# Input tiles outside, token thirds inside, in the first output tile of six late products

## The chip, the cores and the metric
The kernel runs on one core of a Trainium2 chip. The metric is the device time of one execution in microseconds (us); less is better. Engines are named PE (TensorE), DVE (VectorE), ACT (ScalarE), POOL (GpSimd) and SP (SyncE, which issues DMAs here).

## What is computed
One inference step of a hybrid decoder layer over 1024 prompt tokens and 8 sample tokens, 1032 in all, with D = 1024 and a hidden width of 4096. After the two mixers come memory cross-attention and a squared-ReLU MLP, and these last parts are where the change lies:

```python
def cross_attn(h, mk, mv, w_cq, w_co):
    q = (h @ w_cq).reshape(Bsz, L, X_HEADS, X_HEADDIM)
    ...
    return o @ w_co

x = x + merged @ w_out
x = x + cross_attn(rmsnorm(x, g_x), mk, mv, w_cq, w_co)
hf = rmsnorm(x, g_ff) @ w_ff_up
x = x + jnp.square(jax.nn.relu(hf)) @ w_ff_down
```

## The kernel before
Activations are kept transposed: a tensor of 1032 tokens is 8 **input tiles** of 128 channels by 1032 tokens. A product takes a 128x128 block of weights as the stationary operand and writes an **output tile** of 128 channels. Since a PSUM bank holds 512 columns, the 1032 tokens go in three **thirds** of 344, each in its own bank (0, 1, 2). To keep accuracy, weights and activations are both split into a high and a low part, and each product of a weight block and a third is three matmuls (high by high, high by low, low by high: lines 1293, 1294, 1295). An output tile is thus 3 thirds x 8 input tiles x 3 = 72 matmuls, and a product of 8 output tiles is 576.

The late products in program order, all made by `project_all` and its inner `project3`, are named here **CQ** (query projection), **CO** (attention output), and then for each quarter q of the hidden width **FUq** (up) and **FDq** (down), q = 0 to 3. Output tiles are called tile 0 to tile 7 of their product, input tiles go by k = 0 to 7.

- `project3(it, base, before, ...)` makes two output tiles, u = 0 and 1. It waits for the split weights of the tile (`w_split`, from POOL, lines 2768 and 2769). For each third n it waits until the bank has been emptied of the tile before (`before(u, n)`), then goes through k = 0 to 7. The last matmul of a third raises `proj_full`.
- Only tile 0 of a product can meet input tiles that aren't finished yet. `ready(k)` is a semaphore wait for each k, made in the first third; CQ and FU0 have it, on `xl_ready`. FD0 to FD3 instead wait ahead of the whole product until 7 of the 8 hidden tiles are there (`h_ready`, line 1377), and for the eighth at k = 7 (`late`). CO has no such wait.
- `xl_ready` is raised by DVE in `residual_tile` (line 2446: the low part of the scaled residual tile), after adding a square into a running sum (line 2443). `h_ready` is raised by DVE in `low` (line 2600), which ends this chain for hidden tile j: ACT empties the three banks with a ReLU (`relu`, line 1859), DVE scales and squares (`square`, lines 2594 and 2595), ACT makes the high part (`high`, line 1864), DVE the low part.
- The banks of FU are emptied by ACT (`proj_taken`), those of CO and FD by DVE adds into the residual (`sum_taken`, lines 2577 and 2621), those of CQ by ACT.
- In FU0 two small pieces of PE work for the norm stand behind the first and second pair of output tiles (`beside`). Because of the norm, the squares of FU0 begin only after its fourth tile, so that its hidden tiles are finished late, while in FU1 to FU3 they follow each output tile.

Each engine executes its own queue in order, and the matmuls' order is the order in which these loops are written.

Of the kernel before, what the change touches and what calls it, by code (L numbers as in the profile page):

```python
# [11 lines left out]
P = 128  # L12


def wait(eng, sem, value):

    if isinstance(value, int) and value <= 0:
        return
    eng.wait_ge(sem, value)


class Banks:
# [20 lines left out]
    def before(self, name, it=0):  # L43
        b, n = self.place[name]
        return self.base[b] + it * self.per[b] + n
# [9 lines left out]
def rounded(ap):  # L55

    return ap.bitcast(F32R)
# [26 lines left out]
def hybrid_step(nc, io):  # L84
# [10 lines left out]
    KT = D // P  # L95
    NC = T // P
    NG = 3
    GW = NT // NG
# [26 lines left out]
    with ExitStack() as ctx:  # L125
# [6 lines left out]
        def sem(name):  # L132
            return ctx.enter_context(nc.semaphore(name))
# [62 lines left out]
        psum = ctx.enter_context(nc.psum_tensor("psum", [P, 8, 512], F32))  # L196
# [3 lines left out]
        proj_full = sem("proj_full")  # L200
# [34 lines left out]
        sum_taken = sem("sum_taken")  # L235
# [24 lines left out]
        hr_ready, h_ready = sem("hr_ready"), sem("h_ready")  # L260
# [154 lines left out]
        def part(buf, at_, n):  # L415
# [13 lines left out]
        wh, wl = ([wparts[:, (2 * part_ + i) * KT * P:(2 * part_ + i + 1) * KT * P] for i in range(2)]  # L429
                  for part_ in range(2))  # L430
# [23 lines left out]
        hlowv, hiddenv, xFv = (t.rearrange("p (k t) -> p k t", k=KT) for t in (hlow, hidden, xF))  # L454
# [396 lines left out]
        def _(pe):  # L851
# [96 lines left out]
            for n in range(3):  # L948
                hand(setup_plan, f"sc{n}", 0, lambda bk, n=n: (
                    pe.matmul(bk[0:72, 0:GW], wsc[:, k, :], xnv[:, k, n * GW:(n + 1) * GW],  # L950
                              start=(k == 0), stop=(k == KT - 1)) for k in range(KT)))
# [15 lines left out]
            for j in range(2):  # L967
                hand(setup_plan, f"csr{j}", 0, lambda bk, j=j: (
                    pe.matmul(bk[0:40, i * P:(i + 1) * P], tok72[:, 4 * j + i, 0:40], triu[:, :],
                              start=True, stop=True) for i in range(4)))  # L970
# [4 lines left out]
                          start=True, stop=True) for i in range(SH_N // 2)))  # L975
# [254 lines left out]
            with pe.Fori(1, KT // 2) as pair:  # L1230
                j = pair * 2
# [41 lines left out]
                    pe.transpose(cols(bk, 2 * i + t), Ktok[:, t, (2 * q + i) * P:(2 * q + i + 1) * P], ident[:, :])  # L1273
                    for i in range(2) for t in range(MT)))

            def project3(it, base, before, hi, lo, ready=None, late=None):


                for u in range(2):
                    slot = (base + u) % 2  # L1280
                    pe.wait_ge(w_split, it + (base - W_SPLIT + u + 1))
                    for n in range(3):
                        wait(pe, *before(u, n))
                        for k in range(KT):
                            if u == 0 and n == 0:
                                if ready is not None:
                                    pe.wait_ge(*ready(k))
                                if late is not None and k == KT - 1:
                                    pe.wait_ge(*late)
                            w_hi, w_lo = (rounded(w[slot][:, k * P:(k + 1) * P]) for w in (wh, wl))  # L1290
                            x_hi, x_lo = (rounded(x[:, k, n * GW:(n + 1) * GW]) for x in (hi, lo))
                            out = psum[:, n, 0:GW]
                            pe.matmul(out, w_hi, x_hi, start=(k == 0), stop=False)  # L1293
                            pe.matmul(out, w_hi, x_lo, start=False, stop=False)  # L1294
                            mm = pe.matmul(out, w_lo, x_hi, start=False, stop=(k == KT - 1))  # L1295
                        mm.then_inc(proj_full, 1)

            def project_all(base, before, hi, lo, ready=None, late=None, beside=()):
                for i in range(max(1, len(beside))):
                    project3(2 * i, base, lambda u, n: before(2 * i, u, n), hi, lo, ready if i == 0 else None,  # L1300
                             late if i == 0 else None)
                    if beside:
                        beside[i]()
                with pe.Fori(max(1, len(beside)), KT // 2) as pair:
                    j = pair * 2
                    project3(j, base, lambda u, n: before(j, u, n), hi, lo)


            pe.wait_ge(proj_taken, A_CQ)
            project_all(W_CQ, lambda j, u, n: (proj_taken, 3 * j + (A_CQ + 3 * u + n - 2)), xBv, xlowv,  # L1310
                        ready=lambda k: (xl_ready, k + 1))
            pe.wait_ge(q8s_ready, 1)
# [6 lines left out]
            with pe.Fori(0, XH_N) as h:  # L1319
# [10 lines left out]
                for s in range(2):  # L1330
# [10 lines left out]
                    for k in range(2):  # L1341
# [12 lines left out]
                        for k in range(KT) for t in range(MT)))  # L1354
            taken(G, "os1", XH_N - 1)
            project_all(W_CO, lambda j, u, n: (sum_taken, 3 * j + (V_CO + 3 * u + n - 2)), atBv, atv)


# [12 lines left out]
            for q in range(FQ_N):  # L1371
                base, v0, a0 = W_FU + 2 * KT * q, V_FU + V_Q * q, A_END + A_Q * q
                project_all(base, lambda j, u, n: (sum_taken, v0 - 2 + n) if isinstance(j, int) and j + u == 0 else
                            (proj_taken, 3 * j + (a0 + 3 * u + n - 2)), xFv, xlowv,
                            ready=(lambda k: (xl_ready, KT + k + 1)) if q == 0 else None,
                            beside=(ff_sums, ff_spread) if q == 0 else ())
                pe.wait_ge(h_ready, KT * q + KT - 1)
                project_all(base + KT, lambda j, u, n: (proj_taken, a0 + A_Q - 2 + n) if isinstance(j, int) and j + u == 0 else
                            (sum_taken, 3 * j + (v0 + 3 * u + n - 2)), hiddenv, hlowv, late=(h_ready, KT * q + KT))

            pe.wait_ge(xacc_done, 3 * (KT - 1))
            hand(G, "zst", 0, lambda bk: stats([xnv[:, 0, :]], NT, bk, 0, 1))
# [1461 lines left out]
```

## Time and profile before

| | |
|---|---|
| time, median of 3 runs | 3988.59 us (3986.17 to 3994.87) |
| time of the profiled execution | 3986.69 us |
| its span | 3985.0 us |
| PE busy | 3647.3 us (92%), 20671 matmuls |
| DVE, ACT, POOL busy | 43%, 21%, 21% |
| PE on the chain that ended last | 78% |

The span is what the trace covers; the profiled execution's own time is 1.7 us longer. "Busy" is the time an engine spent in instructions. Matmuls are pipelined: a matmul of 0.32 us begins about 0.157 us after the one before it, so that start-to-start distances, not durations, give PE's pace. The granted clock is that which the chip allows TensorE, 1.00 being 2.4 GHz and 0.50 being 1.2 GHz. The late products, from CO on, fill the span from 3098 us to 3955 us; CQ starts at 2812 us.

### The profile page before, as it was taken

How to read it: one execution, taken by the hardware profiler on the slowest of the kernel's cores; microseconds unless marked ns; L12 is line 12 of the kernel's file. 1: busy time of each engine (PE TensorE's matmuls, PEld its weight loads, DVE VectorE, ACT ScalarE, POOL GpSimd, SP SyncE). 2: the span in 40 equal slices, each digit the busy share in tenths (PEclk: the TensorE clock that was granted, in tenths of full speed). 3: DMA queues.
4: the chain of work that ended last, by engine and by line, in shares of the span. 5: the costliest groups of instructions: out<-in, count | busy, mean ns of one | idle time of the engine just before them, and what ended most of it. 6: DMA issues, size and time to landing. Idle time of an engine off the chain costs nothing.

```text
span 3985.0 us, 53368 instructions
## 1 busy us (share of the span) xinstructions
PE 3647.3 (92%) x20671; PEld 3128.8 (79%) x20671; DVE 1693.9 (43%) x2840; ACT 842.6 (21%) x1709; POOL 850.5 (21%) x389
## 2 busy tenths in 40 slices
PE   6899999998899999999999968999988998999998
PEld 5888898887899766666666655667955998999998
DVE  4656555566200356566665760112044232313133
ACT  4333233333211022122221110011123110101010
POOL 3222323232122000000000000000422443444442
PEclk7999999998899998999999979999987999999999
DMA  3111101111222122212222135112312111111111
GB/s 112 45 44 39 32 26 38 43 38 33 75 76 78 54 63 81 81 49 68 66 78 78 43 106 187 54 46 79 128 57 74 43 47 42 43 48 48 43 43 64
DMA packets 317893, 248.31 MB, mean 62 GB/s; under 512 B 11028, under 2 KB 293213, under 8 KB 317717
## 3 DMA queue, kind: packets, MB, share of 16 engines
q1 hardware_dynamic: 282798, 211.28, 17.4%
q10 hardware_dynamic: 34992, 35.58, 2.5%
q8 instruction: 74, 1.21, 0.1%
q14 instruction: 29, 0.24, 0.0%
HBM read 200.50 MB, written 46.78 MB: 62 GB/s over the span
## 4 chain that ended last, share of the span: by engine, by line
PE 78%; DVE 10%; issue 4%; ACT 3%; DMA 2%; POOL 1%; ACTq 0%; DVEq 0%; SPq 0%; POOLq 0%
PE psum L894 22%; PE psum L1293 8%; PE psum L1295 8%; PE psum L1294 8%; PE psum L912 4%; PE psum L913 4%; PE psum L914 4%; PE psum L1028 2%; PE psum L1036 2%; PE psum L1040 2%; PE psum L868 2%; PE psum L1186 1%; PE psum L1324 1%; PE psum L1260 1%; PE psum L1352 1%
## 5 line engine op out<-in xcount | busy, mean ns | idle before, releaser
L894 PE MATMUL psum<-xn,slab 128*128 128x344 f32 x2688 | 823.8, 464 | 29.2 <-ACT arena L1684 17.8
L894 PEld LDWEIGHTS psum<-xn,slab 128*128 128x128 f32 x2688 | 513.5, 194 | 304.0 <-issue 37.6
L2768 POOL TENSOR_SCALAR wparts<-slab 128x1024 fp32r<-128x1024 f32 x80 | 221.9, 2773 | 1001.2 <-POOLq L68 1001.2
L912 PE MATMUL psum<-xh,whe 128*128 128x344 f32 x1152 | 393.4, 341 | 16.2 <-POOL wle L2689 12.8
L913 PE MATMUL psum<-xl,whe 128*128 128x344 f32 x1152 | 373.5, 324 | 0.0
L914 PE MATMUL psum<-xh,wle 128*128 128x344 f32 x1152 | 373.0, 324 | 0.0
L1293 PE MATMUL psum<-at,wparts 128*128 128x344 f32 x960 | 310.8, 324 | 30.0 <-DVE r L2600 26.3
L1295 PE MATMUL psum<-at,wparts 128*128 128x344 f32 x960 | 309.5, 322 | 0.0
L1294 PE MATMUL psum<-xlow,wparts 128*128 128x344 f32 x960 | 307.5, 320 | 0.0
L2689 POOL TENSOR_TENSOR wle<-slab,whe 128x1024 fp32r<-128x1024 f32 x56 | 137.7, 2459 | 721.5 <-ACT whe L1435 721.5
L894 PE MATMUL psum<-arena,slab 128*128 128x344 f32 x768 | 229.1, 460 | 26.6 <-DMA arena<-d_yb 18.5
L1293 PE MATMUL psum<-hB,wparts 128*128 128x344 f32 x768 | 246.7, 321 | 4.5 <-DVE xlow L2446 4.5
L1294 PE MATMUL psum<-r,wparts 128*128 128x344 f32 x768 | 247.4, 322 | 0.0
L1295 PE MATMUL psum<-hB,wparts 128*128 128x344 f32 x768 | 245.7, 320 | 0.0
L912 PEld LDWEIGHTS psum<-xh,whe 128*128 128x128 f32 x1152 | 223.6, 194 | 18.2 <-POOL wle L2689 13.6
L2753 POOL TENSOR_TENSOR arena<-arena 128x1024 f32<-128x1024 f32 x16 | 30.0, 1898 | 972.8 <-DMA arena<-in_state_ssm_dram 972.8
L894 PEld LDWEIGHTS psum<-arena,slab 128*128 128x128 f32 x768 | 148.5, 194 | 105.2 <-issue 31.4
L1916 DVE SCALAR_TENSOR_TENSOR arena<-arena 128x1024 f32<-128x1024 f32 x168 | 224.6, 1337 | 2.7
L913 PEld LDWEIGHTS psum<-xl,whe 128*128 128x128 f32 x1152 | 223.2, 194 | 0.0
L914 PEld LDWEIGHTS psum<-xh,wle 128*128 128x128 f32 x1152 | 221.7, 192 | 0.0
L2769 POOL TENSOR_TENSOR wparts<-slab,wparts 128x1024 fp32r<-128x1024 f32 x80 | 206.5, 2581 | 6.7
L1293 PEld LDWEIGHTS psum<-at,wparts 128*128 128x128 f32 x960 | 183.2, 191 | 31.4 <-DVE r L2600 27.5
(385 smaller groups left out, 6262.0 us busy)
## 6 DMA issues: line engine op xcount, KB each, us to landing
slab<-in_w_in_dram SPq DMA_DIRECT2D x96, 512.0 KB, 4.0
arena<-d_rows SPq DMA_DIRECT2D x40, 512.0 KB, 5.0
slab<-in_w_ff_up_dram SPq DMA_DIRECT2D x32, 512.0 KB, 4.1
slab<-in_w_ff_down_dram SPq DMA_DIRECT2D x32, 512.0 KB, 4.0
out_dram<-arena ACTq DMA_DIRECT2D x24, 512.0 KB, 3.3
d_yb<-arena ACTq DMA_DIRECT2D x16, 516.0 KB, 5.9
arena<-in_state_ssm_dram SPq DMA_DIRECT2D x16, 512.0 KB, 7.1
slab<-in_w_ssm_up_dram SPq DMA_DIRECT2D x16, 512.0 KB, 4.0
```

Source lines behind the costliest of these rows:

```text
L868: yield pe.matmul(bank[:, col + c:col + c + 1], sq[i][:, a:z], ones[:, 0:1], start=(i == 0), stop=(i == k - 1))
L894: mm = pe.matmul(psum[:, n, 0:GW], slabv[(base + u) % 2][:, k, :], src[:, k, n * GW:(n + 1) * GW], start=(k == 0 and u not in join), stop= ...
L912: pe.matmul(out, w_hi, a_hi, start=(k == 0), stop=False)
L913: pe.matmul(out, w_hi, a_lo, start=False, stop=False)
L914: mm = pe.matmul(out, w_lo, a_hi, start=False, stop=(k == KT - 1))
L1293: pe.matmul(out, w_hi, x_hi, start=(k == 0), stop=False)
L1294: pe.matmul(out, w_hi, x_lo, start=False, stop=False)
L1295: mm = pe.matmul(out, w_lo, x_hi, start=False, stop=(k == KT - 1))
L1916: dve.scalar_tensor_tensor(out=y[:, 0:T], in0=x[:, i:i + T], scalar=col[:, 24 + i:25 + i], in1=y[:, 0:T], op0=ALU.mult, op1=ALU.add)
L2689: pool.tensor_tensor(rounded(wle[slot]), slab[slot][:, :], whe[slot], ALU.subtract).then_inc(wlo_ready, 1)
L2768: do(pool.tensor_scalar(rounded(wh[slot]), slab[slot][:, :], 1.0, None, ALU.mult))
L2769: pool.tensor_tensor(rounded(wl[slot]), slab[slot][:, :], wh[slot], ALU.subtract).then_inc(w_split, 1)
```

## The change
`project3` gets another loop order for output tile u = 0 where the caller gives `ready`: input tiles k outside, thirds n inside. The wait for input tile k is made once, ahead of its three thirds; the three bank waits now come within k = 0, ahead of the first matmul in each bank. All three banks are filled at once, and their `proj_full` increments come with the nine matmuls of k = 7. The parameter `late` is gone; FD0 to FD3 no longer wait for 7 hidden tiles ahead of the product, but pass `ready` on `h_ready`, tile by tile. So the new order holds for tile 0 of CQ, FU0, FD0, FD1, FD2 and FD3. All other tiles, and CO, FU1, FU2, FU3 as a whole, keep their order.

```diff
--- before.py
+++ after.py
@@ -1273,32 +1273,31 @@
                     pe.transpose(cols(bk, 2 * i + t), Ktok[:, t, (2 * q + i) * P:(2 * q + i + 1) * P], ident[:, :])
                     for i in range(2) for t in range(MT)))
 
-            def project3(it, base, before, hi, lo, ready=None, late=None):
+            def project3(it, base, before, hi, lo, ready=None):
 
 
                 for u in range(2):
                     slot = (base + u) % 2
                     pe.wait_ge(w_split, it + (base - W_SPLIT + u + 1))
-                    for n in range(3):
-                        wait(pe, *before(u, n))
-                        for k in range(KT):
-                            if u == 0 and n == 0:
-                                if ready is not None:
-                                    pe.wait_ge(*ready(k))
-                                if late is not None and k == KT - 1:
-                                    pe.wait_ge(*late)
-                            w_hi, w_lo = (rounded(w[slot][:, k * P:(k + 1) * P]) for w in (wh, wl))
-                            x_hi, x_lo = (rounded(x[:, k, n * GW:(n + 1) * GW]) for x in (hi, lo))
-                            out = psum[:, n, 0:GW]
-                            pe.matmul(out, w_hi, x_hi, start=(k == 0), stop=False)
-                            pe.matmul(out, w_hi, x_lo, start=False, stop=False)
-                            mm = pe.matmul(out, w_lo, x_hi, start=False, stop=(k == KT - 1))
-                        mm.then_inc(proj_full, 1)
-
-            def project_all(base, before, hi, lo, ready=None, late=None, beside=()):
+                    by_row = u == 0 and ready is not None
+                    for n, k in (((n, k) for k in range(KT) for n in range(3)) if by_row else
+                                 ((n, k) for n in range(3) for k in range(KT))):
+                        if k == 0:
+                            wait(pe, *before(u, n))
+                        if by_row and n == 0:
+                            pe.wait_ge(*ready(k))
+                        w_hi, w_lo = (rounded(w[slot][:, k * P:(k + 1) * P]) for w in (wh, wl))
+                        x_hi, x_lo = (rounded(x[:, k, n * GW:(n + 1) * GW]) for x in (hi, lo))
+                        out = psum[:, n, 0:GW]
+                        pe.matmul(out, w_hi, x_hi, start=(k == 0), stop=False)
+                        pe.matmul(out, w_hi, x_lo, start=False, stop=False)
+                        mm = pe.matmul(out, w_lo, x_hi, start=False, stop=(k == KT - 1))
+                        if k == KT - 1:
+                            mm.then_inc(proj_full, 1)
+
+            def project_all(base, before, hi, lo, ready=None, beside=()):
                 for i in range(max(1, len(beside))):
-                    project3(2 * i, base, lambda u, n: before(2 * i, u, n), hi, lo, ready if i == 0 else None,
-                             late if i == 0 else None)
+                    project3(2 * i, base, lambda u, n: before(2 * i, u, n), hi, lo, ready if i == 0 else None)
                     if beside:
                         beside[i]()
                 with pe.Fori(max(1, len(beside)), KT // 2) as pair:
@@ -1374,9 +1373,8 @@
                             (proj_taken, 3 * j + (a0 + 3 * u + n - 2)), xFv, xlowv,
                             ready=(lambda k: (xl_ready, KT + k + 1)) if q == 0 else None,
                             beside=(ff_sums, ff_spread) if q == 0 else ())
-                pe.wait_ge(h_ready, KT * q + KT - 1)
                 project_all(base + KT, lambda j, u, n: (proj_taken, a0 + A_Q - 2 + n) if isinstance(j, int) and j + u == 0 else
-                            (sum_taken, 3 * j + (v0 + 3 * u + n - 2)), hiddenv, hlowv, late=(h_ready, KT * q + KT))
+                            (sum_taken, 3 * j + (v0 + 3 * u + n - 2)), hiddenv, hlowv, ready=lambda k: (h_ready, KT * q + k + 1))
 
             pe.wait_ge(xacc_done, 3 * (KT - 1))
             hand(G, "zst", 0, lambda bk: stats([xnv[:, 0, :]], NT, bk, 0, 1))
```

In the built program PE has as many instructions as before, and only their order and waits differ; the other engines' instructions are the same.

PE, the first ten matmuls of FD1 (`at` and `r` are the high and the low part of the hidden tiles, `wparts` the split weights), before:

```order
L1293 MATMUL psum<-at,wparts 128x344 [waits proj_taken,w_split,h_ready]
L1294 MATMUL psum<-r_59,wparts 128x344
L1295 MATMUL psum<-at,wparts 128x344
L1293 MATMUL psum<-at,wparts 128x344
L1294 MATMUL psum<-r_59,wparts 128x344
L1295 MATMUL psum<-at,wparts 128x344
L1293 MATMUL psum<-at,wparts 128x344
L1294 MATMUL psum<-r_59,wparts 128x344
L1295 MATMUL psum<-at,wparts 128x344
L1293 MATMUL psum<-at,wparts 128x344
```

and now:

```order
L1292 MATMUL psum<-at,wparts 128x344 [waits h_ready,proj_taken,w_split]
L1293 MATMUL psum<-r_59,wparts 128x344
L1294 MATMUL psum<-at,wparts 128x344
L1292 MATMUL psum<-at,wparts 128x344 [waits proj_taken]
L1293 MATMUL psum<-r_59,wparts 128x344
L1294 MATMUL psum<-at,wparts 128x344
L1292 MATMUL psum<-at,wparts 128x344 [waits proj_taken]
L1293 MATMUL psum<-r_59,wparts 128x344
L1294 MATMUL psum<-at,wparts 128x344
L1292 MATMUL psum<-at,wparts 128x344 [waits h_ready]
```

Lines 1293 to 1295 are now 1292 to 1294. The first three rows are k = 0 in bank 0; the next three were k = 1 in bank 0, and are now k = 0 in bank 1, behind the wait for that bank. The wait on `h_ready` now returns every nine rows, once for each k.

PE, the first matmuls of FU0 (`hB` and `xlow` are the high and the low part of its input), before:

```order
L1293 MATMUL psum<-hB,wparts 128x344 [waits xl_ready,sum_taken,w_split]
L1294 MATMUL psum<-xlow,wparts 128x344
L1295 MATMUL psum<-hB,wparts 128x344
L1293 MATMUL psum<-hB,wparts 128x344 [waits xl_ready]
L1294 MATMUL psum<-xlow,wparts 128x344
L1295 MATMUL psum<-hB,wparts 128x344
L1293 MATMUL psum<-hB,wparts 128x344 [waits xl_ready]
```

and now:

```order
L1292 MATMUL psum<-hB,wparts 128x344 [waits xl_ready,sum_taken,w_split]
L1293 MATMUL psum<-xlow,wparts 128x344
L1294 MATMUL psum<-hB,wparts 128x344
L1292 MATMUL psum<-hB,wparts 128x344 [waits sum_taken]
L1293 MATMUL psum<-xlow,wparts 128x344
L1294 MATMUL psum<-hB,wparts 128x344
L1292 MATMUL psum<-hB,wparts 128x344 [waits sum_taken]
L1293 MATMUL psum<-xlow,wparts 128x344
L1294 MATMUL psum<-hB,wparts 128x344
L1292 MATMUL psum<-hB,wparts 128x344 [waits xl_ready]
```

There `xl_ready` was awaited every three matmuls; it is now awaited every nine, and the two waits between are for banks 1 and 2 of CO's last tile.

## Rows read from the trace of the kernel before

**Rows 1.** The page: share of the chain by engine; the group of POOL L2768.
```profile
PE 78%; DVE 10%; issue 4%; ACT 3%; DMA 2%; POOL 1%; ACTq 0%; DVEq 0%; SPq 0%; POOLq 0%
...
L2768 POOL TENSOR_SCALAR wparts<-slab 128x1024 fp32r<-128x1024 f32 x80 | 221.9, 2773 | 1001.2 <-POOLq L68 1001.2
```

**Rows 2.** Timeline of PE, FU1 tile 0 (columns: start us, us, engine).
```profile
3400.22 0.32 PE L1293 MATMUL psum<-hB,wparts 128*128 128x344 f32 x1
...
3411.54 0.32 PE L1293 MATMUL psum<-hB,wparts 128*128 128x344 f32 x1
```

**Rows 3.** Timeline of PE, FU0 tile 0.
```profile
3191.21 0.32 PE L1293 MATMUL psum<-hB,wparts 128*128 128x344 f32 x1
...
3199.46 0.65 PE L1293 MATMUL psum<-hB,wparts 128*128 128x344 f32 x1 [3.77 <-DVE xlow L2446]
...
3208.93 0.32 PE L1293 MATMUL psum<-hB,wparts 128*128 128x344 f32 x1
```

**Rows 4.** Timeline of DVE as FU0 begins.
```profile
3191.41 0.51 DVE L2577 TENSOR_TENSOR arena<-arena,psum 128x344 f32<-128x344 f32 x1 [3.26 <-PE psum L1295]
...
3198.12 1.28 DVE L2446 SCALAR_TENSOR_TENSOR xlow<-arena,vt,hB 128x1032 fp32r<-128x1032 f32 x1
```

**Rows 5.** Timeline of PE, end of FU0 and FD0 tile 0.
```profile
3292.03 0.32 PE L1295 MATMUL psum<-hB,wparts 128*128 128x344 f32 x1
3307.80 0.66 PE L1293 MATMUL psum<-at,wparts 128*128 128x344 f32 x1 [15.45 <-DVE r L2600]
3308.25 0.49 PE L1294 MATMUL psum<-r,wparts 128*128 128x344 f32 x1
...
3311.12 0.49 PE L1295 MATMUL psum<-at,wparts 128*128 128x344 f32 x1
...
3320.98 0.32 PE L1293 MATMUL psum<-at,wparts 128*128 128x344 f32 x1
```

**Rows 6.** Timeline of DVE, low parts of hidden tiles 3 to 7.
```profile
3293.83 1.23 DVE L2600 TENSOR_TENSOR r<-arena,at 128x1032 fp32r<-128x1032 f32 x1 [5.59 <-ACT at L1864]
...
3299.41 1.22 DVE L2600 TENSOR_TENSOR r<-arena,at 128x1032 fp32r<-128x1032 f32 x1
...
3302.96 1.23 DVE L2600 TENSOR_TENSOR r<-arena,at 128x1032 fp32r<-128x1032 f32 x1
...
3306.52 2.44 DVE L2600 TENSOR_TENSOR r<-arena,at 128x1032 fp32r<-128x1032 f32 x2
```

**Rows 7.** Timeline of PE, tile 0 of FD1, FD2 and FD3.
```profile
3490.78 0.32 PE L1293 MATMUL psum<-at,wparts 128*128 128x344 f32 x1
...
3493.92 0.32 PE L1295 MATMUL psum<-at,wparts 128*128 128x344 f32 x1
3497.87 0.42 PE L1293 MATMUL psum<-at,wparts 128*128 128x344 f32 x1 [3.63 <-DVE r L2600]
...
3505.98 0.32 PE L1293 MATMUL psum<-at,wparts 128*128 128x344 f32 x1
...
3675.78 0.32 PE L1293 MATMUL psum<-at,wparts 128*128 128x344 f32 x1
...
3692.54 0.32 PE L1293 MATMUL psum<-at,wparts 128*128 128x344 f32 x1
...
3862.34 0.32 PE L1293 MATMUL psum<-at,wparts 128*128 128x344 f32 x1
...
3880.01 0.32 PE L1293 MATMUL psum<-at,wparts 128*128 128x344 f32 x1
```

**Rows 8.** Timeline of ACT, then of DVE, at the start of FD1.
```profile
3491.07 0.46 ACT L1859 ACTIVATE arena<-psum 128x344 f32 x1 [3.31 <-PE psum L1295]
...
3495.84 1.97 DVE L2600 TENSOR_TENSOR r<-arena,at  x1 [1.33 <-ACT at L1864]
```

**Rows 9.** Timeline of PE, CQ tile 0.
```profile
2812.30 0.40 PE L1293 MATMUL psum<-at,wparts 128*128 128x344 f32 x1 [3.71 <-issue]
...
2825.22 0.32 PE L1293 MATMUL psum<-at,wparts 128*128 128x344 f32 x1
```

## The prediction

> **What bounds the kernel now.** I read the page's chain first: PE carries 78% of it [rows 1]. So I look for time in which PE stands. PE's timeline at the start of each late product shows it. An undisturbed tile 0, that of FU1, takes 3411.54 - 3400.22 = 11.32 us from its first matmul to tile 1's [rows 2], which is 72 matmuls at 0.157 us. Whatever a tile 0 takes above 11.32 us is a wait for input or a slower clock.
>
> - FU0: 3208.93 - 3191.21 = 17.72 us [rows 3]. It stands until 3199.46 for the last tile's low part (3198.12 + 1.28 = 3199.40, so a release takes about 0.06 us) [rows 4], and the first matmuls after it last up to 0.65 us rather than 0.32.
> - FD0: FU0's last matmul starts at 3292.03, so FD0 could start at 3292.19. It starts at 3307.80 and its tile 0 ends at 3320.98 [rows 5]: 28.79 us where 11.32 would do.
> - FD1: 3505.98 - 3490.78 = 15.20 us; FD2: 16.76; FD3: 17.67 [rows 7]. Each does k = 0 to 6 of the first third, 21 matmuls, and then stands for input tile 7, in FD1 until 3497.87.
> - CQ: 12.92 us, but with no gap inside after its start [rows 9]; the 1.6 us above 11.32 are the clock after an idle start.
>
> **The change, part by part.** Work is neither added nor removed: 72 matmuls in each tile 0, in another order. Before, PE came to input tile k after 3k matmuls, now after 9k. So input tile 7 is needed 63 x 0.157 = 9.9 us after the start rather than 3.3.
>
> FU0: input tile 6 is needed at 3191.21 + 54 x 0.157 = 3199.69, tile 7 at 3201.1. Even tile 7 is there at 3199.46 [rows 4]. No stall is left, the clock has no reason to fall, and tile 0 takes 11.32: **gain 17.72 - 11.32 = 6.4 us**.
>
> FD1 to FD3: input tile 7 is finished at 3495.84 + 1.97 + 0.06 = 3497.87 [rows 8] and needed at 3490.78 + 9.90 = 3500.68, with 2.8 us to spare. All three stalls go: **(15.20 - 11.32) + (16.76 - 11.32) + (17.67 - 11.32) = 3.9 + 5.4 + 6.4 = 15.7 us**. The difference between the three was the clock: after the same stall it stayed up in FD1 and fell in FD2 and FD3.
>
> FD0: its input is really late, so here a part stays. The low parts of tiles 3 to 7 end at 3295.06, 3300.63, 3304.19, 3307.74 and 3308.96 [rows 6]; the two last are one merged row, cut in half. PE can now start at 3292.19, has done tiles 0 to 3 (36 matmuls) at 3297.84, and then takes each tile 0.06 us after its low part: tile 4 at 3300.69, tile 5 at 3304.25, tile 6 at 3307.80, 1.41 us each at full clock, and tile 7 directly after tile 6, at 3309.21. At full clock tile 0 ends at 3310.6, a gain of 10.4 us. But PE then works 1.4 us and stands about 2.1 to 2.8 us, three times over, and after a stall of 3.6 us the clock had fallen in two of three products [rows 7]. I take the half clock, at 0.287 us a matmul ((3311.12 - 3308.25) / 10 [rows 5]), which lasts for about 12 matmuls after the last stall, as it did in this very place before: 3307.80 + 12 x 0.287 + 6 x 0.157 + 0.1 = 3312.3. **Gain 3320.98 - 3312.3 = 8.7 us**. With 18 matmuls at half clock it would be 8.0; both ends, 8.0 and 10.4, are kept for the range.
>
> CQ: all of its input is there when it starts; nothing is gained, and the slow clock at its start stays: 0.
>
> New waits. (a) Bank 2 is now wanted 6 matmuls after the start rather than 48: in FD1 at 3490.78 + 0.94 = 3491.72. ACT leaves the bank at 3491.07 + 0.46 + 0.06 = 3491.59 [rows 8]. In FU0 it is wanted at 3192.15, and DVE leaves it at 3191.41 + 0.51 + 0.06 = 3191.98 [rows 4]. Both are in time, by 0.13 and 0.17 us. (b) At the end of tile 0 the three banks fill together, and tile 1 wants bank 0 at once. Bank 0's last matmul starts 7 x 0.157 = 1.10 us before tile 1's first. The bank's release came 0.97 us after a last matmul with ACT (3491.59 against a last matmul at 3490.62, which is 3490.78 - 0.16) and, by the same count in FU0, 0.93 us with DVE. So it is free 0.13 to 0.17 us ahead. Cost of (a) and (b): 0. If each release cost PE what it did in FD0 at half clock, 0.45 us to the next matmul where 0.29 is usual [rows 5], it would be 12 x 0.16 = 1.9 us for six products; that is the lower end, and a gain from these waits is excluded, since none of them takes another's place. (c) The bank now changes every 3 matmuls instead of every 24. The 20 distances that FD1 covers within one bank take 3493.92 - 3490.78 = 3.14 us [rows 7], 0.157 each, the same as FU1's 72 with three changes of bank [rows 2]. I take 0; the rivals price it. (d) The extra waits on `ready` in FD find their semaphores raised. CQ has such a wait before every k of its first third already, and its 1.6 us above 11.32 are no more than 12 matmuls at half clock give (12 x 0.13) [rows 9]. 0.
>
> What is behind: POOL splits a tile's weights when the tile two before it is done, and the first two tiles' weights are split under the previous product, so tile 0's earlier end brings the later splits forward with it. In FU0 ACT's and DVE's work on hidden tiles follows PE, and moves as a block.
>
> Sum: 6.4 + 15.7 + 8.7 = 30.8 us. Everything after these products hangs on PE, so it passes to the end: 3986.7 - 30.8 = 3955.9 us for the profiled execution. The median of the runs shown is 1.9 us above that execution, so **3957.8, rounded 3958 us**.
>
> **The rivals.**
>
> *The clock falls where the banks rotate (slower).* If in each new tile 0 PE ran at 1.2 GHz, because it goes round three banks with a hand-over in each, tile 0 would take 72 x 0.287 = 20.7 us. Then FU0 costs 20.7 - 17.72 = +3.0, FD0 20.7 - 28.79 = -8.1 (at that pace it finds every input tile finished), FD1 +5.5, FD2 +3.9, FD3 +3.0, CQ 20.7 - 12.92 = +7.8: in all +15.1 us, a median of 4003.7. The whole swing is 30.8 + 15.1 = 45.9 us, so it decides once about two thirds of these matmuls run at half clock. Against it: FU1 goes through three banks with no sign of a pause [rows 2], and nothing in the new order makes PE stand between matmuls. The Trainium skill, "TensorE: Matmul & The Clock Gate", section "A second HAM failure mode: psum-queue depth-cycling", describes a kernel that cycled through PSUM banks in each iteration and whose clock went up and down; by that rule the change would be a loss. No row here has such a pattern at three matmuls a bank. Chance 0.03.
>
> *Each change of bank costs a little.* The nearest row is again the 0.16 us after a release [rows 5]. Tile 0 has 21 more changes of bank than before, in six products 126. At half of that each, 0.08, the gain shrinks by 10 us to 21: 3968; at the whole of it, by 20 us to 11: 3978. At 0.18 us or more it would be lost in the noise. Against it stand the equal distances of rows 2 and 7. Chance 0.05.
>
> *The stalls only move.* If after tile 0 something else were late, say the third tile's weights, which POOL begins when tile 0 ends and for which SP needs a free slab, the gain would come back as idle time in tile 1 or 2. POOL's first instruction for a tile takes 2773 ns [rows 1] and the second, a subtraction of the same size, not more; 5.6 us at most stand against 11.32 us of a tile, so I see no room for it. Should most of the gain go this way, the time is within 8 us of before, about 3984. Chance 0.04.
>
> **How the numbers follow.** The forecast holds with 0.88. Its gains go from 6.4 + 15.7 + 8.0 - 1.9 = 28.2 to 6.4 + 15.7 + 10.4 = 32.5 us. Against the runs shown, 3986.2 to 3994.9, that is 3953.7 to 3966.7. I give **3952 to 3967**, which leaves out the rivals and a little of the forecast. A measurement of this kernel can tell about 0.2%, 8 us, from no change: faster 0.93 (the forecast and the bank price), same 0.04, slower 0.03. My forecast is 0.77% faster.
>
> **What the changed profile would show.** Tile 0 of FU0, FD1, FD2 and FD3 takes 11.3 us each, with no idle time of PE before an L1292 matmul that waits for `xlow` or `r`, and a granted clock of 1.00. FD0 shows three short waits for `r` of about 2 to 3 us in place of one of 15.45, and its tile 0 ends about 20 us after FU0, not 29. PE's busy time changes little. The first ReLU or add after each tile 0 comes as a burst of three. Wrong would be: idle time before tile 1 of these products (the banks), distances above 0.157 us within the rotating part (a price of the change of bank), a clock of 0.50 there with no stall before it, or a wait for `w_split` in tile 2.

## The result, and the profile after

| | before | after |
|---|---|---|
| median of 5 runs | 3986.17 us (3982.92 to 3994.87) | 3956.06 us (3939.94 to 3957.79) |
| profiled execution, span | 3985.0 us | 3950.8 us |
| PE busy | 3647.3 us | 3638.9 us |

The ratio of after to before is 0.9911, with a 95% interval from 0.9888 to 0.9934. The change is faster, as forecast. The median of after is inside my range of 3952 to 3967 us; the ratio applied to the median of before gives 3950.7 us, which is 1.3 us under its low end. So the direction held, and by the ratio the gain, 35.5 us, came out larger than the 30.8 us I had worked out. This result alone doesn't tell the two apart: the interval of the ratio goes from 26 to 45 us, and the two medians are 30.1 us apart. That the median of after comes within 2 us of the 3958 forecast is in part the luck of five runs that spread over 18 us.

The page of after, the chain's shares by engine and the group to which the largest stalls of the late products belonged; the last row is the same group on the page of before:

```profile
PE 74%; DVE 9%; issue 8%; ACT 3%; POOL 2%; DMA 2%; ACTq 0%; DVEq 0%; SPq 0%; POOLq 0%
...
L1292 PE MATMUL psum<-at,wparts 128*128 128x344 f32 x960 | 308.8, 322 | 9.3 <-DVE r L2598 5.2
...
L1293 PE MATMUL psum<-at,wparts 128*128 128x344 f32 x960 | 310.8, 324 | 30.0 <-DVE r L2600 26.3
```

That group's idle time is down from 30.0 to 9.3 us, and DVE's low part now ends 5.2 us of it, where it ended 26.3. PE's share of the chain reads 74% instead of 78% [rows 1], with more put down as issue; I traced no part of that to the late products. From FU0 until 9 us behind FD3, PE has only these two waits (columns: who waited for whom, us in total, times, longest):

```profile
PE psum L1292 <- DVE r L2598: 5.2, 3, 2.8
PE psum L868 <- DVE xn L2441: 4.2, 1, 4.2
```

The first is FD0, in three pieces. The second belongs to the final norm, behind FD3, and is as it was before. Waits in FU0, FD1, FD2 and FD3 are gone. Ahead of FU0, the 5.5 us that PE stands before CO's first matmul are as before. PE's timeline of after in FU0, the first matmul of tile 0 and of tile 1 (start us, us, engine, line):

```profile
3189.57 0.32 PE L1292 MATMUL psum<-hB,wparts 128*128 128x344 f32 x1
...
3200.85 0.32 PE L1292 MATMUL psum<-hB,wparts 128*128 128x344 f32 x1
```

The same in FD0, with the last matmul ahead of the first wait and the first matmul behind each of the three:

```profile
3284.10 0.32 PE L1292 MATMUL psum<-at,wparts 128*128 128x344 f32 x1
...
3289.59 0.32 PE L1294 MATMUL psum<-at,wparts 128*128 128x344 f32 x1
3292.66 0.65 PE L1292 MATMUL psum<-at,wparts 128*128 128x344 f32 x1 [2.76 <-DVE r L2598]
...
3296.22 0.42 PE L1292 MATMUL psum<-at,wparts 128*128 128x344 f32 x1 [0.61 <-DVE r L2598]
...
3299.77 0.42 PE L1292 MATMUL psum<-at,wparts 128*128 128x344 f32 x1 [1.87 <-DVE r L2598]
...
3302.74 0.40 PE L1292 MATMUL psum<-at,wparts 128*128 128x344 f32 x1
```

And in FD1, the first matmul of tile 0 and of tile 1:

```profile
3472.63 0.32 PE L1292 MATMUL psum<-at,wparts 128*128 128x344 f32 x1
...
3483.97 0.40 PE L1292 MATMUL psum<-at,wparts 128*128 128x344 f32 x1
```

FU0's tile 0 takes 11.28 us where it took 17.72 [rows 3]. FD0 starts right behind FU0 and its tile 0 ends 18.64 us later, where it took 28.79 from FU0's end [rows 5]. FD1's takes 11.34 where it took 15.20 [rows 7]; FD2's and FD3's are 11.34 and 11.32. DVE's low parts of hidden tiles 3 to 7, which answer to [rows 6], and the adds of FD0's tile 0:

```profile
3285.74 1.23 DVE L2598 TENSOR_TENSOR r<-arena,at 128x1032 fp32r<-128x1032 f32 x1 [5.58 <-ACT at L1862]
...
3291.39 1.22 DVE L2598 TENSOR_TENSOR r<-arena,at 128x1032 fp32r<-128x1032 f32 x1
...
3294.94 1.23 DVE L2598 TENSOR_TENSOR r<-arena,at 128x1032 fp32r<-128x1032 f32 x1
...
3298.49 2.44 DVE L2598 TENSOR_TENSOR r<-arena,at 128x1032 fp32r<-128x1032 f32 x2
3302.08 1.45 DVE L2619 TENSOR_TENSOR arena<-arena,psum 128x344 f32 x3 [1.14 <-PE psum L1294]
```

Their distances are 5.65, 3.55 and 3.55 us, where they were 5.58, 3.55 and 3.56; DVE did not become faster, PE only no longer waits for all of them. The last row is the burst of three adds at the end of tile 0. The granted clock of PE's three bursts in FD0 (columns: stretch, its length, busy us and instructions of PE, PEld, DVE, ACT and POOL, granted clock, DMA share, GB/s) was 0.50, 1.00 and 1.00:

```profile
3292.60:3295.50 2.90, 2.83 (x9) 2.50 (x9) 2.87 (x4) 0.45 (x1) 0.00 (x0) 0.50 0.43 130
3296.20:3297.90 1.70, 1.68 (x9) 1.40 (x9) 1.67 (x2) 0.00 (x0) 0.00 (x0) 1.00 0.00 0
3299.80:3302.80 3.00, 3.00 (x19) 2.88 (x19) 1.86 (x3) 0.00 (x0) 0.00 (x0) 1.00 0.00 0
```

### The profile page after: what moved, and what is told of

Its sections match the earlier page's. It is cut to its first block, busy times and chain, and to the rows that moved or that the text cites. A ratio compares the mean times of both kernels' runs of the same rounds, so it can differ in the third digit from the quotient of the medians.

```text
span 3950.8 us, 53368 instructions
## 1 busy us (share of the span) xinstructions
PE 3638.9 (92%) x20671; PEld 3120.4 (79%) x20671; DVE 1690.2 (43%) x2840; ACT 843.3 (21%) x1709; POOL 852.6 (22%) x389
## 4 chain that ended last, share of the span: by engine, by line
PE 74%; DVE 9%; issue 8%; ACT 3%; POOL 2%; DMA 2%; ACTq 0%; DVEq 0%; SPq 0%; POOLq 0%
PE psum L894 22%; PE psum L1292 8%; PE psum L1294 8%; PE psum L1293 8%; PE psum L912 3%; PE psum L913 3%; PE psum L914 3%; PE psum L1028 2%; PE psum L1036 2%; PE psum L1040 2%; PE psum L868 2%; POOL wle L2687 1%; PE psum L1260 1%; PE psum L1323 1%; PE psum L1186 1%
## 5 line engine op out<-in xcount | busy, mean ns | idle before, releaser
L894 PE MATMUL psum<-arena,slab 128*128 128x344 f32 x768 | 229.1, 460 | 26.6 <-DMA arena<-d_yb 18.6
L2751 POOL TENSOR_TENSOR arena<-arena 128x1024 f32<-128x1024 f32 x16 | 30.1, 1900 | 970.4 <-DMA arena<-in_state_ssm_dram 970.4
L1399 ACT ACTIVATE arena<-psum 128x512 f32<-128x512 f32 (+5 forms) x242 | 112.6, 479 | 444.8 <-PE psum L1028 251.3
```

What stands on the lines that cost most here:

```text
L894: mm = pe.matmul(psum[:, n, 0:GW], slabv[(base + u) % 2][:, k, :], src[:, k, n * GW:(n + 1) * GW], start=(k == 0 and u not in join), stop= ...
L1399: act.activation(dst, src(got(plan, name, it)), func, **kw).then_inc(bank_taken[plan.bank(name)], 1)
```

## The experiments

All kernels ran beside the kernel before on the same chip. Where a time of tile 0 is given, it is from the first matmul of tile 0 to that of tile 1, and for FD0 it is counted from the place at which FU0 ended.

**The changed kernel again.** No edit.

> The changed kernel once more, unaltered, to pin the size of its gain. If its late products alone made the difference, the time from FU0's first matmul to the end is 32.6 us shorter than in the kernel before (761.2 against 793.8 us in the two profiled executions), and the median should be about 32 us lower. The rival is that the change does something in the first 3190 us too: then the median is 35 us or more lower and FU0 starts 1.5 us or more earlier again.

Measured: median 3954.60 us against 3990.37 us, ratio 0.9908 (0.9893 to 0.9923). From FU0's first matmul to the end of the span it took 761.8 us, in the first profile of after 761.2. But the medians are 35.8 us apart and not 32.6, while FU0's first matmul came at 3193.99 us in this profile, not earlier than the 3191.21 us of before. Neither expectation fits: the missing 3 us don't show in the first 3190 us of after. PE's three stalls in FD0 were 2.76, 1.88 and 1.86 us, and none of the bursts behind them began at half clock (0.42 to 0.43 us for the first matmul); tile 0 took 18.66 us, as in the first profile, 18.64:

```profile
3297.09 0.42 PE L1292 MATMUL psum<-at,wparts 128*128 128x344 f32 x1 [2.76 <-DVE r L2598]
...
3300.65 0.43 PE L1292 MATMUL psum<-at,wparts 128*128 128x344 f32 x1 [1.88 <-DVE r L2598]
...
3304.20 0.43 PE L1292 MATMUL psum<-at,wparts 128*128 128x344 f32 x1 [1.86 <-DVE r L2598]
```

The kernel before had to be looked at again.

**The kernel before, profiled twice more.** No edit.

> The kernel before, profiled again. The changed kernel's local gain by the profiles is 32.6 us, that by medians 35.8. Theory: before, the clock after each stall falls in some executions and not in others, and in the first profile it had stayed up in FD1 and recovered soon in FU0 and FD2; so another execution should show a longer tile 0 in FU0 (up to 19.0 us, as in the kernel with a wait for each tile) or in FD1 and FD2 (up to 17.7 us). Rival: the tile 0 times are the same 17.7, 28.8, 15.2, 16.8, 17.7 us again, and the difference comes from the first 3190 us.

> The kernel before, profiled a third time; as for the second: with the clock as the cause, tile 0 of FU0, FD1, FD2 and FD3 varies between executions by up to 2.5 us each; with the first 3190 us as the cause, it is the same and FU0's first matmul starts at another time.

Measured: 3993.25 and 3988.37 us. FU0's tile 0 took 19.03 and 19.01 us, FD0's tile 0 29.5 in both, FD1's 17.84 and 17.85, FD2's 17.89 and 17.88, FD3's 17.90 and 17.92. In the profile that I had read they were 17.72, 28.79, 15.20, 16.76 and 17.67. The stretch from FU0 to the end was 799.6 us in both and 793.8 in mine. PE's timeline of the second execution in FD1, tile 0's first matmul, the first after the stall, and tile 1's first:

```profile
3493.50 0.32 PE L1293 MATMUL psum<-at,wparts 128*128 128x344 f32 x1
...
3500.59 0.65 PE L1293 MATMUL psum<-at,wparts 128*128 128x344 f32 x1 [3.63 <-DVE r L2600]
...
3511.34 0.32 PE L1293 MATMUL psum<-at,wparts 128*128 128x344 f32 x1
```

The stall is the same 3.63 us as in [rows 7], but the first matmul behind it takes 0.65 us where it took 0.42, and the granted clock of the four microseconds behind it is 0.50, that is 1.2 GHz (the third column from the end):

```profile
3500.60:3504.60 4.00, 4.00 (x14) 4.00 (x15) 0.51 (x1) 0.00 (x0) 0.00 (x0) 0.50 0.46 131
```

So a stall may cost more than its length, by an amount that varies between executions, and the stretch from FU0 on was 5.8 us shorter in the profiled execution that I read than in these two. This is shown. How often either case occurs is not: the kernel that only waits tile by tile, the next experiment, has the same stalls in FD1 to FD3, and its profile shows the short times of the first profile again (15.20, 16.76 and 17.70 us). FU0 started at 3191.9 and 3187.1 us in the two, which is the other part of the scatter, without a cause that I tested.

**Only the waits, not the order.** On top of the changed kernel:

```diff
-                    by_row = u == 0 and ready is not None
+                    by_row = False
...
-                        if by_row and n == 0:
+                        if u == 0 and n == 0 and ready is not None:
```

> Thirds stay outside as before, but FD0 to FD3 wait for each hidden tile in its turn. Theory (the order matters, since it delays the need for input tile 7 from 3.3 to 9.9 us): FD1, FD2, FD3 and FU0 keep their stalls (tile 0 of 15.2 to 17.7 us), FD0 can use tiles 0 to 6 early in its first third only, and its tile 0 ends 26.4 us after FU0 instead of 28.8 (24.9 if the clock stays up). Whole gain against the kernel before 2 to 4 us. Rival (the wait for 7 tiles at once was the cost): most of the 31 us are gained here too.

Measured: median 3984.94 us against 3990.37, ratio 0.9986 (0.9976 to 0.9995), 5.6 us faster by the ratio, with an interval of 2 to 10 us, where 2 to 4 was expected. FU0's tile 0 took 19.03 us, FD1's 15.20, FD2's 16.76, FD3's 17.70, as in the kernel before; FD0's took 26.87 us against the 26.4 worked out. PE's first matmuls after each stall of FD0:

```profile
3300.67 0.43 PE L1292 MATMUL psum<-at,wparts 128*128 128x344 f32 x1 [1.35 <-DVE r L2598]
...
3306.24 0.66 PE L1292 MATMUL psum<-at,wparts 128*128 128x344 f32 x1 [4.83 <-DVE r L2598]
...
3309.80 0.66 PE L1292 MATMUL psum<-at,wparts 128*128 128x344 f32 x1 [2.33 <-DVE r L2598]
...
3313.35 0.66 PE L1292 MATMUL psum<-at,wparts 128*128 128x344 f32 x1 [2.33 <-DVE r L2598]
```

PE waits for input tiles 3, 4, 5 and 6 in turn, with a third of the work to do on each, and from the second stall on each burst begins at half clock (0.66 us). The waits one by one bring FD0 1.9 to 2.6 us. Tile 0 of the five products together is 0.6 us shorter than in the first profile of before and 6.6 us shorter than in the other two; of these, 2.6 are FD0's and 4.0 the clock in FD1 to FD3, whose order is that of before. The loop order brings the rest of the gain. The rival, most of 31 us, falls.

**Only two thirds alternate.** On top of the changed kernel:

```diff
-                    for n, k in (((n, k) for k in range(KT) for n in range(3)) if by_row else
+                    for n, k in ([(n, k) for k in range(KT) for n in range(2)] + [(2, k) for k in range(KT)] if by_row else
```

> As the changed kernel, but in tile 0 only thirds 0 and 1 alternate, and third 2 comes after them, so that input tile 7 is needed 42 x 0.157 = 6.6 us after the start and not 9.9. Theory: in FD1 to FD3 it is ready 7.1 us after the start, so each has a stall of 0.5 to 0.6 us and a tile 0 of 11.9 us; in FU0 the stall is 1.65 us and tile 0 takes 13.0 us; FD0's tile 0 ends 21.6 us after FU0 at full clock, up to 23.2 with the clock down. Gain against the kernel before 4.7 + 5.6 to 7.2 + 13.9 = 24 to 26 us. Rival (any rotation is enough): the same tile 0 as in the changed kernel, 11.3 us, and the same gain.

Measured: median 3962.11 us against 3990.37, ratio 0.9929 (0.9913 to 0.9946), so 28.3 us where 24 to 26 was expected. That expectation was counted against the first profile of before, against which tile 0 of the five products is 23.7 us shorter; against the other two it is 29.7. FU0's tile 0 took 13.12 us (13.0 expected), FD1's, FD2's and FD3's 11.97, 11.98 and 11.98 (11.9 expected), FD0's 23.42 (21.6 to 23.2 expected; its three bursts all began at half clock). PE's rows behind the stalls of FU0, FD1, FD2 and FD3:

```profile
3198.45 0.42 PE L1292 MATMUL psum<-hB,wparts 128*128 128x344 f32 x1 [1.52 <-DVE xlow L2444]
...
3486.91 0.42 PE L1292 MATMUL psum<-at,wparts 128*128 128x344 f32 x1 [0.37 <-DVE r L2598]
...
3668.67 0.42 PE L1292 MATMUL psum<-at,wparts 128*128 128x344 f32 x1 [0.37 <-DVE r L2598]
...
3850.46 0.43 PE L1292 MATMUL psum<-at,wparts 128*128 128x344 f32 x1 [0.37 <-DVE r L2598]
```

In FD1 the matmul that needs input tile 7 starts at 3486.91 us instead of 3479.75 + 6.60 = 3486.35, 0.56 us late, where the expectation had 0.5 to 0.6. In these four products the place of the need for the last input tile against the time at which it is ready accounts for tile 0 to about 0.1 us. Behind their short stalls the clock stayed up: the first matmul takes 0.42 or 0.43 us, and only one start-to-start distance in each tile 0 is above 0.2 us besides the stall. FD0's 23.42 us are above the 21.6 worked out for full clock.

**All output tiles rotate.** On top of the changed kernel:

```diff
-                    by_row = u == 0 and ready is not None
+                    by_row = True
...
-                        if by_row and n == 0:
+                        if u == 0 and n == 0 and ready is not None:
```

> The changed kernel with input tiles outside and thirds inside in every output tile of CQ, CO, FU0 to FU3 and FD0 to FD3: 74 tiles more, each with 21 more changes of bank, 1554 more in all. Theory (a change of bank costs nothing, only the hand-over at a tile's end does): tile 1 of FD0 to FD2 took 11.41 us in the changed kernel, 0.09 more than usual, so the other tiles after a rotated one cost 0.03 to 0.1 us each, 2 to 8 us in all; inside a tile the distance stays 0.157 us and the clock stays 1.00; besides, the last hidden tile comes 0.9 us later, which FD1 to FD3 have room for and FD0 has not. About 3957 to 3963 us. Rival 1 (a price per change of bank): 0.02 us each would be 31 us, so 3985 us or more. Rival 2 (the clock falls where banks rotate): half clock in the late products, hundreds of us slower.

Measured: median 3951.25 us against 3990.96, ratio 0.9909 (0.9884 to 0.9933), the same as the changed kernel's. Two stretches in which every output tile rotates, of FU1 and of FD1 (columns as above):

```profile
3390.00:3470.00 80.00, 80.00 (x511) 79.92 (x510) 33.84 (x21) 17.94 (x30) 39.00 (x14) 1.00 0.16 46
3480.00:3560.00 80.00, 80.00 (x509) 79.39 (x508) 10.28 (x22) 0.00 (x0) 36.17 (x14) 1.00 0.16 46
```

PE is busy throughout and the clock is 1.00, 2.4 GHz. FD1 as a whole took 90.81 us against 90.66 in after, FU1 90.53 against 90.56, FD3 90.24 against 90.57. With 147 more changes of bank in each of FD1 and FD3 the difference is between -0.33 and +0.15 us, so a change of bank costs nothing that can be seen. Both rivals fall, the slower one of the prediction too. The 3957 to 3963 us expected were too slow: a rotated tile of FD3 takes 11.28 us and not 11.32, and against it the other tiles of FD1 take 0.05 to 0.1 us more, which is the allowance for a hand-over, so that the two nearly cancel. From FU0's first matmul to the end it took 763.2 us, 1.5 to 2.0 more than the changed kernel.

The expectation also had the last hidden tile come 0.9 us later. It didn't: its low part ended 16.83 us after FU0 in this kernel and in the changed one. Yet FD0's tile 0 took 20.41 us instead of 18.64. PE's first matmuls after its stalls show the clock:

```profile
3287.91 0.42 PE L1292 MATMUL psum<-at,wparts 128*128 128x344 f32 x1 [2.76 <-DVE r L2598]
...
3291.47 0.66 PE L1292 MATMUL psum<-at,wparts 128*128 128x344 f32 x1 [1.33 <-DVE r L2598]
...
3295.02 0.65 PE L1292 MATMUL psum<-at,wparts 128*128 128x344 f32 x1 [0.60 <-DVE r L2598]
```

With the same order and the same input times in this tile, the slow clock costs 1.8 us here and nothing in the two profiles of the changed kernel.

**Only FD1, FD2 and FD3.** A parameter `rows` switches the order off for CQ, FU0 and FD0, which keep thirds outside and wait tile by tile:

```diff
-                    by_row = u == 0 and ready is not None
+                    by_row = u == 0 and ready is not None and rows
...
-                            (sum_taken, 3 * j + (v0 + 3 * u + n - 2)), hiddenv, hlowv, ready=lambda k: (h_ready, KT * q + k + 1))
+                            (sum_taken, 3 * j + (v0 + 3 * u + n - 2)), hiddenv, hlowv, ready=lambda k: (h_ready, KT * q + k + 1), rows=q > 0)
```

> The new loop order in FD1, FD2 and FD3 alone; CQ, FU0 and FD0 keep thirds outside (with a wait for each input tile in its turn). Theory: the parts are independent, so FD1 to FD3 take 11.3 us each for tile 0 and give 15.7 us against the profiled execution of before, FU0 keeps its stall (17.7 to 19.0 us), and FD0 is as in the kernel that only waits tile by tile, 26.9 us, 2 us better than before; in all 17 to 18 us, and a few more against the median of before if the clock usually falls in FD1 too. Rival (FU0's or FD0's earlier start is what helps FD1 to FD3): they keep part of their stalls.

Measured: median 3967.84 us against 3990.96, ratio 0.9945 (0.9926 to 0.9964), 22 us, where 17 to 18 and a few more were expected. FD1, FD2 and FD3 took 11.35, 11.35 and 11.32 us for tile 0, FU0 kept 19.01 and FD0 26.87. Against the second and third profile of before, tile 0 of the five products sums to 102.2 - 79.9 = 22.3 us less, and the medians are 23.1 us apart. The parts add up; nothing is passed from FU0 or FD0 to the later ones.

**Two high parts at a time, on top of the changed kernel.** What is left in FD0 is 18.64 - 11.32 = 7.3 us. ACT makes the high parts of FU0's first four hidden tiles one by one, each behind the ReLU of a later tile, and four are left for the end.

```diff
             for j in range(4, KT):
                 relu(j, 0)
-                high(j - 4, 0)
-            for j in range(4, KT):
-                high(j, 0)
+                high(2 * (j - 4), 0)
+                high(2 * (j - 4) + 1, 0)
```

> On top of the changed kernel, ACT makes two high parts of hidden tiles after each of FU0's tiles 4 to 7, instead of one and then four in a row at the end. Theory: what is left of FD0's stall (tile 0 takes 18.6 us where 11.3 would do) is the backlog that ACT's order leaves for DVE; DVE needs 3.7 to 5.7 us a tile and has 11.3, so it catches up, the last low part ends about 7 us after FU0, FD0's tile 0 takes 11.3 to 11.5 us, and the kernel is 7.3 us faster than the changed one. Rival: ACT, waiting for DVE's squares, empties FU0's banks late, so PE stands in FU0's tiles 5 to 7 for some us each; then FU0 grows by what FD0 loses and the time stays.

Measured: median 3946.54 us against 3990.37, ratio 0.9888 (0.9874 to 0.9903). FD0's tile 0 takes 11.31 us, without a wait, and FU0 keeps its 11.28 us and 83.26 us for the other tiles. From FU0's first matmul to the end it took 754.6 us, 6.6 to 7.2 less than the two profiles of the changed kernel. The timeline of this kernel, first the last low parts on DVE (two in one row), then PE's first matmuls of FD0's tile 0 and tile 1:

```profile
3288.35 4.59 DVE L2597 TENSOR_TENSOR r<-arena,at 128x1032 fp32r<-128x1032 f32 x2
```

PE:

```profile
3284.69 0.32 PE L1292 MATMUL psum<-at,wparts 128*128 128x344 f32 x1
...
3296.00 0.40 PE L1292 MATMUL psum<-at,wparts 128*128 128x344 f32 x1
```

The last low part ends at 3292.94 us, 8.25 us after FU0 (about 7 expected), and is needed 9.9 us after it. The rival falls: PE doesn't stand in FU0's later tiles. This is the fastest kernel of the study. The medians on the same chip are 8.1 us apart (3954.60 and 3946.54), and all five of its runs (up to 3947.11) are shorter than all five of the changed kernel there (from 3948.99). The intervals of the two ratios overlap, so the size, 7.3 us expected, rests on the traces more than on the times.

**Two high parts at a time, alone.** The same edit, in the kernel before.

> The kernel before, with ACT's order of two high parts after each of FU0's tiles 4 to 7 and nothing of the changed loop order. Theory (FD0's stall has two causes, ACT's backlog and PE's early need, and either cure alone takes the same part): by the trace of the run with both, the low parts of tiles 6 and 7 end 6.0 and 8.3 us after FU0, so FD0 starts 6.0 us after FU0 and its tile 0 ends at 6.0 + 11.3 + 1.6 to 2.5 us of slow clock = 19 to 20 us after FU0, where before it was 28.8 to 29.5. FU0, FD1, FD2 and FD3 stay as they were. Gain 9 to 10 us, so the sum of the two alone (10 and about 36) is about 2 us above what both gave together. Rival (the gains are independent): as much as both together gave on top of the new loop order, 7.3 us, and no more.

Measured: median 3982.09 us against 3988.80, ratio 0.9984 (0.9967 to 1.0), 6.4 us with an interval of 0 to 13, which alone would not settle it. FD0's tile 0 ended 20.2 us after FU0 (19 to 20 expected), against 29.5 in the second and third profile of before, so the trace gives 9.3 us. FU0, FD1, FD2 and FD3 took 19.00, 16.77, 17.95 and 17.94 us. PE's first matmul of FD0:

```profile
3299.49 0.65 PE L1293 MATMUL psum<-at,wparts 128*128 128x344 f32 x1 [6.92 <-DVE r L2599]
```

The stall is 6.92 us where it was 15.45 [rows 5]; FD0 starts 7.1 us after FU0, where 6.0 was expected. From 29.5 us the loop order alone takes FD0's tile 0 to 18.6, the high parts alone to 20.2, and both together to 11.3. That is 10.9, 9.3 and 18.2 us: the two overlap by 2.0 us, as expected, and otherwise take separate parts, the one PE's early need and the other ACT's backlog. The rival, 7.3 us in either place, is off by 2 us in the trace; the times alone could not tell the two apart.

## Why the prediction was right, and where it was wrong

- **FU0, 6.4 us.** Measured 17.72 - 11.28 = 6.44 against the execution that I read. No clock fell and no stall was left, as worked out.
- **FD1 to FD3, 15.7 us.** Measured 3.86 + 5.42 + 6.35 = 15.6 against that execution, with the input tile needed after its time, not before. The kernel in which two thirds alternate confirms the reckoning, at 6.6 us instead of 9.9.
- **FD0, 8.7 us.** Measured 28.79 - 18.64 = 10.15 us. The step that failed here is my choice of half clock for the 12 matmuls after the last stall. In after only the first of the three bursts ran at half clock (0.65 us for its first matmul, 0.42 for the other two), and it cost nothing, because the next input tile was later still. In the second profile of after no burst did, and tile 0 took the same. The full-clock bound, 10.4, was the right one. In the kernel in which all tiles rotate, two bursts began at half clock, the last among them, and FD0 took 20.41 us, close to the 20.1 that I had worked out: my case exists, it was not this one.
- **Sum.** 6.44 + 15.6 + 10.15 = 32.2 us measured, for a forecast of 30.8.
- **From the profiled execution to the median.** This is the step that put the gain too low and the range's low end too high. I wrote that after the same stall the clock "stayed up in FD1 and fell in FD2 and FD3", took the tile 0 times of that one execution as those of the kernel, and carried only the 1.9 us between it and the median. In two further profiles the clock fell in all of them, and longer in FU0 and FD0: 19.02 + 29.50 + 17.84 + 17.89 + 17.91 = 102.2 us against the 96.1 I used. The changed kernel has 63.9 us for the same five, in both of its profiles. So the gain is 32.2 us against one execution and 38.2 against the others, and the two measured ratios, 0.9911 and 0.9908, which make 35.5 and 36.7 us, lie in between. Their intervals, 26 to 45 and 31 to 43 us, hold both ends, so how much of the clock's share the median has is not shown. A term for the clock, 0 to 6 us, was missing from the sum and from the low end; with it the range would have begun at 3946.
- **New waits (a) to (d), 0.** Nearly right: tile 1 of FD0, FD1 and FD2 takes 11.40 to 11.41 us, 0.09 more than usual, and tile 0 of FD1 and FD2 0.02 more, so about 0.3 us in all. FD3, whose adds are written out rather than in a loop with computed addresses, shows nothing; whether that is the reason was not tried. The upper bound of 1.9 us was generous.
- **CQ, 0.** 12.91 us against 12.92.
- **The slower rival** had 0.03 and falls with the kernel in which every tile rotates: the clock is 1.00 through whole products. The pattern that the Trainium skill describes in "TensorE: Matmul & The Clock Gate", section "A second HAM failure mode: psum-queue depth-cycling", short idles of PE between groups of matmuls and a clock that goes up and down, does not appear here: PE is busy for 80.00 of 80 us in both stretches. **The price of a change of bank** had 0.05 and is nil in the same run. **That stalls only move** had 0.04; none appeared, in tile 1 or in tile 2.

What stays open: why the clock stays up after one stall of 3.63 us and falls after another of the same length, how often it does either, and what moves FU0's first matmul between 3187 and 3195 us in kernels that are the same up to there.

## What to carry to other kernels

Where the last input of a product arrives late, put the loop over inputs outside and the loop over independent output pieces inside, for the first output tile only: with three pieces the need for the last input came three times as late here, 9.9 us after the start instead of 3.3, at no cost that the runs show, each piece having a bank of its own. Compute the time at which each input is needed against that at which it is ready, tile by tile; that reckoning held to about 0.1 us here wherever the clock stayed up. And price a PE stall at its length plus the slow matmuls behind it, taken from several executions rather than from one.

## What the runs showed of the hardware that I had not expected

- One and the same stall of 3.63 us before an identical stream of matmuls cost tile 0 either 3.9, 5.4 or 6.4 to 6.6 us above 11.32: nothing, about 1.6 us or 2.4 to 2.7 us for the clock. All three levels occur in one profile of the kernel before (15.20, 16.76, 17.67 us), in FD1, FD2 and FD3, and again in that of the kernel that only waits tile by tile; the highest occurs in all three places in the two other profiles of before.
- FD0's tile 0 has the same order and the same input times in the changed kernel and in the one in which all tiles rotate. After stalls of 2.76, 1.88 and 1.86 us every burst began at full clock; after 2.76, 1.33 and 0.60 us the last two began at half clock. The clock fell within the first of these bursts (granted 0.67 over it), and the stalls behind it are shorter because PE came to them later.
- Alternating three PSUM banks every three matmuls runs at the pace of one bank for 24: 0.157 us per matmul over whole products (90.24 to 90.81 us for 576 against 90.56 to 90.67), clock 1.00.
